# Experts with column halves of the expert weights as stationary operand, 96 rows per block, and a slot table built by one-hot matmuls

## What is computed

```python
g_top, g_idx = lax.top_k(softmax(h @ w_rg + b_rg), 1)        # one of 4 groups
e_top, e_idx = lax.top_k(e_logits[group], 2)                 # two of its 8 experts
e_w = softmax(e_top) * g_top
# for every expert e, over the rows routed to it
y = (silu(x @ w_gate[e]) * (x @ w_up[e])) @ w_down[e]        # 1024 -> 256 -> 1024
out[row] += y * weight
```

## Time and profile before

| | us |
|---|---|
| median of 3 runs | 1850.72 |
| lowest and highest | 1848.87, 1853.21 |
| the profiled execution | 1846.78 |
| its span, first to last instruction | 1845.0 |
| merge, from its first to its last instruction | 1199 to 1397 |
| slots | 1401 to 1436, with its last transfers landing after that |
| experts | 1442 to 1845 |

### The profile page before, as it was taken

How to read it: one execution, slowest core, us unless ns; L and a number is a source line. 1 busy time by engine, 2 the same in 40 slices (tenths; PEclk the granted TensorE clock), 3 DMA queues, 4 the chain that set the end, 5 groups by cost and what they waited for, 6 DMA issues and landing times. The chain is left out here.

```text
span 1845.0 us, 30700 instructions
## 1 busy us (share of the span) xinstructions
PE 1605.4 (87%) x12312; PEld 1037.5 (56%) x12312; DVE 883.4 (48%) x1874; ACT 450.8 (24%) x873; POOL 110.0 (6%) x131
## 2 busy tenths in 40 slices
PE   4999999659999999999994888759981599999994
PEld 3888888525666666666663555525540244444442
DVE  2454645536566666666663666526663122222221
ACT  2222222222222322332211333324540011111110
POOL 0000000000000000000000000000003222222221
PEclk9999999879999999999995999979995799999997
DMA  9322321262231231221104344244526499999982
GB/s 330 118 85 80 113 97 63 83 227 74 71 118 58 78 111 48 78 78 53 59 24 132 102 88 88 64 177 161 201 85 237 148 368 368 365 365 373 373 296 38
DMA packets 103630, 280.20 MB, mean 152 GB/s; under 512 B 31776, under 2 KB 50336, under 8 KB 94032
## 3 DMA queue, kind: packets, MB, share of 16 engines
q1 hardware_dynamic: 93680, 244.78, 37.6%
q0 software_dynamic: 9824, 33.63, 7.2%
HBM read 209.45 MB, written 68.98 MB: 151 GB/s over the span
## 5 line engine op out<-in xcount | busy, mean ns | idle before, releaser
L1069 PE MATMUL b_ps<-b_wg,b_hT 128*128 128x512 f32 x576 | 277.7, 615 | 29.6 <-DMA b_wg<-w_gates 29.3
L1986 PE MATMUL f_hidden<-wgu,f_xT 128*128 128x512 f32 x512 | 225.7, 594 | 0.0
L505 PEld LDWEIGHTS a_ps<-a_hT,a_wz 128*128 128x128 f32 x1792 | 202.6, 192 | 3.8 <-issue 3.8
L505 PE MATMUL a_ps<-a_hT,a_wz 128*128 128x128 f32 x1792 | 204.0, 275 | 0.0
L1069 PEld LDWEIGHTS b_ps<-b_wg,b_hT 128*128 128x128 f32 x576 | 101.4, 191 | 124.7 <-issue 119.9
L1986 PEld LDWEIGHTS f_hidden<-wgu,f_xT 128*128 128x128 f32 x512 | 97.7, 191 | 122.5 <-issue 122.5
L1753 PE MATMUL d_ps<-wo,d_oT 128*128 128x512 f32 x288 | 130.8, 603 | 0.8 <-DVE d_oT L1588 0.8
L2003 PE MATMUL f_down<-wd,f_midT 128*128 128x512 f32 x256 | 116.9, 600 | 1.0 <-DVE f_midT L2023 1.0
L1422 PE MATMUL c_score<-c_kT,c_qT 96*128 96x512 f32 (+2 forms) x192 | 76.2, 508 | 24.5 <-DMA c_v<-v_d 24.5
L2023 DVE COPY f_midT<-f_midps 128x256 f32<-128x256 f32 x32 | 13.6, 425 | 162.7 <-PE f_midps L1993 162.7
L1753 PEld LDWEIGHTS d_ps<-wo,d_oT 128*128 128x128 f32 x288 | 53.4, 192 | 59.4 <-issue 57.8
(11 more groups left out here) (308 smaller groups left out, 2474.6 us busy)
## 6 DMA issues: line engine op xcount, KB each, us to landing
wgu<-w_gate_up SPq DMA_DIRECT2D x32, 2048.0 KB, 13.7
wd<-w_down SPq DMA_DIRECT2D x32, 1024.0 KB, 6.7
b_hT<-hT_d SPq DMA_DIRECT2D x36, 512.0 KB, 4.1
gate_d<-b_logits SPq DMA_DIRECT2D x36, 256.0 KB, 2.6
d_gate<-gate_d SPq DMA_DIRECT2D x9, 1024.0 KB, 5.8
b_wg<-w_gates SPq DMA_DIRECT2D x4, 2048.0 KB, 12.7
zm_d<-a_zm SPq DMA_DIRECT2D x9, 896.0 KB, 4.6
b_zm<-zm_d SPq DMA_DIRECT2D x9, 896.0 KB, 6.5
```

The costliest lines, as they stand in the source:

```text
L505: mm = pe.matmul(banks[Z_BANKS[n % 2]][:, j * P:(j + 1) * P], wz[:, i, (g + j) * P:(g + j + 1) * P], hT[t % 2][:, i, :], start=(i == 0), s ...
L1069: mm = pe.matmul(banks[FILL][:], hT[q % 2][:, k, :], wg[u % 2][:, k, :], start=(k == 0), stop=(k == DC - 1))
L1986: mm = pe.matmul(hidden[b][:], xT[b][:, k, :], wgu[wb][:, k, :], start=(k == 0), stop=(k == DC - 1))
```

## The change

`CAP` goes from 128 to 96, and three things are rebuilt.

**The arithmetic of an expert.** In `up` the weights are stationary and the rows move: for each 128 columns of gate (2 such groups) and of up (2), each of 8 chunks, and each half of 64 columns, one matmul with 96 moving rows. The two halves write to partitions 0 to 63 and 64 to 127. The product comes out with the hidden dimension on the partitions, so `turn_mid` and its copy go. ACT starts on the gate half (`gate_done`) before the up half is there. `xT` is copied with 96 instead of 128 columns per chunk, and gather and add move 96 rows.

**The table.** `record` in merge compares each row's place with the numbers 0 to 95 (`at_place`), makes `told` (token number and weight, one-hot by expert), and `place_rows` on PE adds their product to a table [96 places x 64] one tile later. `finish_table` closes it after the last tile. POOL gathers the rows of the first two experts at the end of merge. The stage `slots` is gone; its arithmetic for overflow blocks is cut in 8 parts that DVE does after experts 2 to 9 (`place_overflow`), and the 18 scatters are spread over experts 10 to 27 on POOL.

**The weights.** There are five buffers instead of four. Three experts' weights are loaded during merge (tiles 1 to 3), the other two at the start of `experts`. merge waits for 10 constants instead of 7. `OVERFLOW` goes from 16 to 22.

```diff
-CAP = P
+CAP = 96
-WB = 4
+WB, WB_EARLY = 5, 3
+EARLY = 2
@@ merge, SP
             for t in range(NT):
+                if 1 <= t <= WB_EARLY:
+                    e = t - 1
+                    sp.dma_start(keep["wgu"][e][:], io["w_gate_up"][ORDER[e]])...
+                    sp.dma_start(keep["wd"][e][:], io["w_down"][ORDER[e]])...
@@ merge, POOL
+            for j in range(2):
+                pool.wait_ge(h2_stored[j], 16 * ((NT + 1 - j) // 2))
+            pool.wait_ge(rows_known, 1)
+            for e in range(EARLY):
+                pool.tensor_copy(index[e][:], row_of[:, ORDER[e]:ORDER[e] + 1]).then_inc(index_set, 1)
...
+                pool.indirect_dma_start(xg[e][:], None, io["h2_d"]...)
@@ merge, DVE, record(n)
+                if n >= 1:
+                    dve.tensor_tensor(table[:], table[:], banks[7][0:CAP, P:P + 2 * NE], ALU.add)
...
+                dve.tensor_tensor(at_place[:], spread(places[:].unsqueeze(1), [P, 2, CAP]), ..., ALU.is_equal)
+                dve.tensor_scalar(told[:, :, 0, :], hot(n), token[:, n:n + 1], None, ALU.mult)
+                dve.tensor_tensor(told[:, :, 1, :], hot(n), ..., ALU.mult).then_inc(told_ready, 1)
+            def finish_table():
+                step(dve.scalar_tensor_tensor(empty[:], run[0:CAP, :], token[0:CAP, 0:1], nobody[0:CAP, :], ALU.is_le, ALU.mult))
+                dve.wait_ge(table_done, 1)
+                step(dve.tensor_tensor(table[:], table[:], banks[7][0:CAP, P:P + 2 * NE], ALU.add))
+                dve.tensor_tensor(row_of[:], table[:, 0:NE], empty[:], ALU.add).then_inc(rows_known, 1)
@@ merge, PE
+                if n >= 1:
+                    mm = place_rows(n - 1)
+            def place_rows(n):
+                pe.wait_ge(told_ready, n + 1)
+                for k in range(2):
+                    mm = pe.matmul(banks[7][0:CAP, P:P + 2 * NE], at_place[:, k, :], told[:, k], start=(k == 0), stop=(k == 1))
@@ experts, PE, up
-            for k in range(DC):
-                mm = pe.matmul(hidden[b][:], xT[b][:, k, :], wgu[wb][:, k, :], start=(k == 0), stop=(k == DC - 1))
-            mm.then_inc(s["up_done"], 1)
+            for part, flag in enumerate(("gate_done", "up_done")):
+                bank = (gated, upped)[part][b]
+                for f in range(FB):
+                    cols = slice(f * CAP, (f + 1) * CAP)
+                    for k in range(DC):
+                        for half in HALVES:
+                            mm = pe.matmul(bank[half, cols], wgu[wb][:, k, (part * FB + f) * P:(part * FB + f + 1) * P][:, half],
+                                           xT[b][:, k, :], start=(k == 0), stop=(k == DC - 1))
+                mm.then_inc(s[flag], 1)
@@ experts, SP
+            for e in range(WB_EARLY, WB):
+                load_up(e)
+                load_down(e)
@@ experts, POOL
                 if e + AHEAD < NE:
-                    gather(pool, s, e + AHEAD, e % AHEAD, (e + AHEAD) % (2 * AHEAD), ORDER[e + AHEAD])
+                    gather(e + AHEAD)
+                if 0 <= e - 10 < 2 * NT:
+                    scatter(e - 10)
@@ experts, DVE
+                if 2 <= e < 10:
+                    place_overflow(e - 2)
```

406 lines of the change are left out of this document (206 added, 200 removed).

## The result

| | median | lowest to highest | runs | profiled execution (span) |
|---|---|---|---|---|
| before | 1850.78 us | 1848.87 to 1853.21 | 4 | 1846.78 (1845.0) us |
| after | 1817.56 us | 1816.55 to 1819.19 | 4 | 1819.19 (1817.4) us |

The ratio is 0.9821, with a 95% interval of 0.9804 to 0.9838. The change makes the kernel faster by 33 us, 1.8%. The forecast was 82 us, 1769, and 1817.56 lies outside its range of 1752 to 1800. The sign was right and more than half of the gain is missing. The profiled execution is the slowest of the four, 1.6 us over their median.

A forecast was written before the change was run, and what follows sets the result against it. It took PE and the full transfer engines, both at about 11.4 us an expert, plus a 53 us hole as bounds. 1845.0 - 39.8 + 4.0 - 60 + 10 + 4.5 = 1763.7 us span, forecast 1769, range 1752 to 1800.

The forecast's parts named there:

- 5, the end: After the last add: six more empty turns of the overflow loop, +4.5 us.
- Term 1: Between merge and the first expert: PE's idle gap shrinks from 53.0 to 13.2 us, -39.8.
- Term 2: In merge: the added table-building instructions on PE and new constants cost +4.0 us; preloaded weights cost nothing.
- Term 3: PE's work per expert: 85 ns a pair of half matmuls, period 9.54 us, -60 us in all.
- C: In `up`: column halves don't overlap at 96 rows, a pair takes at least 170 ns, 1931 us; chance 0.03.
- B: In `up`: a pair of halves takes 110 ns, period 11.1 us, transfers hidden, 1807 us; chance 0.06.
- E: Experts and merge: no stall at all and merge hides its additions, 1755 us or a little less; chance 0.11.
- Term 4: Transfers in the experts: 114.4 MB to move, so PE waits for gate and up weights near the end, +10 us.
- At what rate?: Transfer rate in the experts: took 372 GB/s, so 114.4 MB need 307 us.
- So it holds, barely: Gathers in the expert loop: 10.2 us to land fits the 10.7 us left, with perhaps a few waits of a microsecond.
- A: Transfers in the experts bind harder: 1783 us at 358 GB/s, up to 1800 with more gather waits; chance 0.14.
- D: Expert loop stays at 11.4 us as full transfer engines gain nothing from fewer rows, near 1813 us; chance 0.06.

The follow-up runs named there:

- The floor kernel: Changed kernel with gathers issued ahead of the adds, plus w_down loads from the sixth on cut to 128 of 1024 columns: 1762.75 us.
- the best kernel: Changed kernel with gathers issued ahead of the adds and gathers of 128 rows, adds staying at 96: 1775.91 us, ratio 0.9601 to before.

## Why the prediction was wrong, point by point

The terms of the sum, as the traces have them. Where merge begins is seen in PE's first transposes, before and after:

```profile
1218.32 1.97 PE L1746 MATMUL d_ps<-d_ident,d_o 128*128 128x128 f32 x8 [22.77 <-DMA d_real<-real]
```

```profile
1222.70 1.97 PE L1786 MATMUL d_ps<-d_ident,d_o 128*128 128x128 f32 x8 [22.78 <-DMA d_nobody<-nobody]
```

| term | forecast | in the trace of after |
|---|---|---|
| stages ahead of merge | 0 | +4.4 |
| 1, the hole | -39.8 | -35.5 |
| 2, merge | +4.0 | +2.9 |
| 3 and 4, the experts | -60 + 10 = -50 | -2.7 |
| 5, the end | +4.5 | +3.3 |
| sum of the span | -81.3 | -27.6 |

**Stages ahead.** 1222.70 - 1218.32 = 4.4 us in this one execution. In the other kernels made from after they stand between 1216.5 and 1224.1 us, so 4.4 us are within what executions differ by. It also explains why the spans differ by 27.6 us and the medians by 33.2: the profiled execution of before was 3.9 us under its median, that of after 1.6 over.

**Term 1** was right in kind and 4.3 us too large. The step that was short is the change of stage, 4.7 us in the sum and 9.0 in the trace. "The gathers cost nothing more" was wrong at exactly that place: the last one is issued by 1410.85 and the DRAIN ends at 1414.2, 3.3 us later, and from there the change takes 5.6 us.

**Term 2** was right. From merge's first transposes to the end of its last reduction it takes 1404.20 - 1222.70 = 181.5 us, where before had 1396.89 - 1218.32 = 178.6. PE is at 116.98 busy of 120 us. The weights queued into merge raise the share from 0.50 to 0.69 and delay nothing.

**Term 3's price was right.** 84 ns a pair where I had 85, a period of 9.68 where I had 9.54. The steps from the earlier trace rows, how much the rows and how much the weight load make of a pair, hold at 96 rows and at 128 (111 ns). So C is refuted here, and with it the Trainium skill's rule on row groups in "TensorE: Matmul & The Clock Gate", section "The mechanism", which I had weighed at 190 ns a pair: both halves use all 128 rows and the pair takes 84 ns. B, with 110 ns, is refuted too. E, no stall at all, needed the transfers to keep up, and they did not. The floor kernel, which keeps all this and takes the transfers away, stands at 1762.8.

**Term 4 failed, in two steps.** The first is the sentence "At what rate?". I took 372 GB/s from rows in which the gathers had 128 rows or there were none, and used it for gathers of 96. With those the engines give 337 to 348 GB/s. My own sum gives the price: 114.4 MB take 307.5 us at 372 GB/s and 338.5 at 338, which is 31 us. With these and the 4.3 us of term 1 the forecast would have been 1769 + 31 + 4 = 1804, and the kernel with the gathers first, where only the weights are waited for, has 1803.7. The same sum for gathers of 128 rows is 114.4 + 30 x 0.131 = 118.3 MB at 385 GB/s, 307.4 us, so 1773, and 1772.2 and 1775.9 were measured. The rates in these two sums come from the windows of the same kernels, so they check the budget of bytes and the way from rate to time, not the rate. What I took for one rate whatever is transferred goes with the form of the gather.

The second step is "So it holds, barely". 0.75 x 13.6 = 10.2 us for a gather was right for the old loop: in the kernel before with 96 rows they landed after 9.1 to 10.4 us. In the new loop those into `f_xg` take 13.8 to 16.0 and those into `xg` 10.4 to 15.1, with medians of 14.5 and 14.0. The loads beside them land later as well, w_gate_up after 17.1 us instead of 11.5. That PE frees the buffers of weights earlier, so that more loads are under way when a gather is issued, fits with this; no run tests it alone. 10.7 us were left. This cost 13.9 us, the difference that the order makes at 96 rows. The waits are only a part of what it costs: 34.6 us of waits and 19 of lower clock go when the gathers are early, but only 13.9 of these 53.8 show in the time: the rest comes back in front of the weights, which bind next.

**The rivals.** A named both mechanisms, engines that bind and gathers that are waited for, and priced them at 1783 to 1800; its gathers were under-priced and its rate of 358 GB/s was still too high. D named the outcome, a loop that stays near 11.4 us "since what full transfer engines give isn't changed by fewer rows", at 1813. After's period is 11.53 us, and 128 rows instead of 96 leave its time where it is; D is the nearest of all. I gave D 0.06, since nothing in the rows of before showed it; the share of 1.02 spoke for it and I took it for a price by the byte. No rival had the form of the gathers as its cause. The limit that the Trainium skill's page "DMA: Bandwidth & Descriptors", section "Specifications", gives for HBM per core, some 358 GB/s, does not explain either regime: 385 GB/s over 220 us are above it and 338 below.

**Open** is why one gather of 128 rows goes better with the loads beside it than one of 96 or 112. The same page's section "Why a DMA increments its semaphore by 16 and not by 1" says that tiles of 128 and of 96 partitions are both spread over all 16 engines. The traces agree in so far as the share is 1.01 to 1.02 with both. By the number of engines alone one rate would be expected, and the table above shows 338 and 385.

## What to carry to other kernels

A rate read in a full window holds for the transfers in that window: if the change alters the form of one of them, treat the rate as unknown and bound it, and if the rest of the loop is at the rate, that unknown is the forecast. A share of 1.0 is no measure of room; look at the time from issue to landing, which here grew when PE became faster. And when PE gains from fewer rows, the transfers need not follow. In this kernel the best choice was to gather 128 rows even where 96 are used, to add 96, and to issue the gathers ahead of whatever waits for a result of the same expert; elsewhere, try both counts for both transfers.

## What the runs showed of the hardware that was not expected

- Gathers of 4 KB rows beside loads of 1 and 2 MB: with 128 rows in one instruction the sixteen engines moved 364 to 385 GB/s at a share of 1.01 to 1.02, with 96 or 112 rows 337 to 348, and with 128 rows as 96 + 32 only 341. For adds into HBM it is not so: with 128-row gathers, adds of 96 rows went with 385 GB/s and adds of 128 with 375, and with 96-row gathers 337 and 348. In time the 128-row adds cost 35.6 and 7.5 us.
- Beside 96-row gathers the loads of weights slow down themselves: 43.9 us of an engine's time a MB instead of 38.1.
- GpSimd's DRAIN at the end of a block took 4.49 us behind two gathers just issued and 0.04 us without.
- The longer instruction was the faster kernel: 0.13 MB more for every expert took 27.8 us off the time (1803.7 to 1775.9).
- A pair of matmuls with 64 weight columns each, in the two column halves, takes 84 ns with 96 moving rows and 111 ns with 128, its weight loads hidden. It is as fast a row as the whole array with 128 columns, and not faster.
- After 10 of the 11 waits of 2.6 to 3.9 us the granted clock fell to 0.5, and the next product took mostly 5.29 us instead of 3.60; after one wait of 2.80 us it stayed at 1.00. Of 53.8 us lost in the experts of after, 18.2 were this.
- With many small matmuls there are pauses of up to 2.3 us in the middle of a group, in which PE waits for nothing that the profile shows: 14.1 us in all with 96-row gathers first, 5.7 in the best kernel, and 1.2 where most of w_down was left out. They go with the queue of loads rather than with the rate: the kernel without early gathers moves 384 GB/s, has w_gate_up landing after some 30 us instead of 38, and has none. That they are instructions being fetched is a guess that no run tested.
